# Expert weights of a mixture layer: another order of loads on SyncE's queue, w2 in runs of four rows, w1 and w3 read with a stride

## The reference

```
z      = modulate(rms_norm(tokens)) @ w_in          # S5 | differential attention | latent attention
x      = x + g_m * (concat(s5, diff, mla) @ w_out)
h      = modulate(rms_norm(x))                      # 512 tokens
group  = argmax(h @ w_group);  experts = top 2 of 8 in that group, weights w
out    = sum over the 2 experts of a token: w * ((silu(h @ w1[e]) * (h @ w3[e])) @ w2[e])
result = rms_norm(x + g_f * out)
```

## Time and profile before

| | |
|---|---|
| median of 3 runs | 1286.86 us (1285.66 to 1292.4) |
| profiled execution | 1281.67 us |
| its span, first to last instruction | 1279.9 us |
| mean granted TensorE clock | 0.888 |
| PE (TensorE matmul) busy | 960.2 us, 75% |
| PEld (weight load) busy | 453.2 us, 35% |
| DVE (VectorE) busy | 422.1 us, 33% |
| ACT (ScalarE) busy | 246.7 us, 19% |
| POOL (GpSimd) busy | 159.9 us, 12% |
| DMA moved | 264.89 MB, mean 207 GB/s |

### The profile page before, as it was taken

How to read it: one execution, slowest core, us unless ns; L and a number is a source line. 1 busy time by engine, 2 the same in 40 slices (tenths; PEclk the granted TensorE clock), 3 DMA queues, 4 the chain that set the end, 5 groups by cost and what they waited for, 6 DMA issues and landing times.

```text
span 1279.9 us, 11562 instructions
## 1 busy us (share of the span) xinstructions
PE 960.2 (75%) x3837; PEld 453.2 (35%) x3837; DVE 422.1 (33%) x1062; ACT 246.7 (19%) x529; POOL 159.9 (12%) x401
## 2 busy tenths in 40 slices
PE   4589999877999989963955577567777777777780
PEld 2245554653444544451422233222222222222220
DVE  2337656635777541350101111011111111111115
ACT  3411002123455541110100000001111111111102
POOL 5010100110000000003001100112122211121112
PEclk8799999878899999965977788789999999999985
DMA  9831211230516700040355433599999999999975
GB/s 306 309 113 60 34 66 66 38 92 7 208 56 229 133 1 16 33 148 20 148 216 218 184 123 134 222 404 392 398 392 377 376 379 406 382 341 377 392 277 202
DMA packets 61234, 264.89 MB, mean 207 GB/s; under 512 B 11496, under 2 KB 13856, under 8 KB 42256
## 3 DMA queue, kind: packets, MB, share of 16 engines
q1 hardware_dynamic: 48256, 246.04, 50.4%
q0 software_dynamic: 12768, 18.36, 5.7%
q10 hardware_dynamic: 176, 0.05, 0.0%
HBM read 266.22 MB, written 22.31 MB: 225 GB/s over the span
## 4 chain that ended last, share of the span: by engine, by line
issue 45%; PE 35%; DVE 6%; DMA 4%; POOL 4%; ACT 3%; POOLq 1%; SPq 0%; DVEq 0%; ACTq 0%
PE PS L679 9%; PE PS L906 4%; PE PS L837 3%; DMA W<-in_w_mod 3%; PE PS L814 3%; PE PS L971 2%; POOL held L526 2%; PE PS L588 2%; PE PS L638 2%; PE PS L825 1%; DVE sml L1671 1%; PE PS L747 1%; PE PS L740 1%; POOL S5R L535 1%; ACT MP L1175 1%
## 5 line engine op out<-in xcount | busy, mean ns | idle before, releaser
L968 PE MATMUL PS<-W,S5R 128*64 128x512 f32 x800 | 193.1, 628 | 63.9 <-DMA W<-in_moe_w 63.8
L679 PE MATMUL PS<-W,HTR 128*128 128x512 f32 (+2 forms) x352 | 143.9, 567 | 3.2 <-DVE MP L1398 3.2
L971 PE MATMUL PS<-W,S5R 128*128 128x512 f32 x192 | 94.4, 654 | 62.6 <-DMA W<-in_moe_w 60.2
L988 PE MATMUL PS<-W,S5R 128*64 128x512 f32 x400 | 101.9, 656 | 51.6 <-ACT S5R L1255 32.3
L968 PEld LDWEIGHTS PS<-W,S5R 128*64 128x64 f32 x800 | 57.0, 143 | 197.3 <-DMA W<-in_moe_w 99.1
L1248 ACT ACTIVATE S5R<-PS 128x256 f32<-128x256 f32 (+1 forms) x31 | 13.2, 425 | 520.5 <-PE PS L968 369.5
L679 PEld LDWEIGHTS PS<-W,HTR 128*128 128x128 f32 x352 | 66.6, 198 | 71.5 <-issue 67.9
L526 POOL TENSOR_TENSOR held<-held 1x1 f32<-1x1 f32 x147 | 26.9, 183 | 484.1 <-PE PS L953 164.3
L1905 DVE TENSOR_TENSOR S5R<-S5R,PS 128x256 f32<-128x256 f32 x25 | 10.5, 422 | 228.8 <-ACT S5R L1248 228.8
L971 PEld LDWEIGHTS PS<-W,S5R 128*128 128x128 f32 x192 | 40.0, 212 | 113.6 <-DMA W<-in_moe_w 61.8
L1917 DVE TENSOR_TENSOR S5R<-PS,QKV 64x512 f32<-64x512 f32 x50 | 34.4, 688 | 131.3 <-PE PS L988 130.5
(11 more groups left out here) (398 smaller groups left out, 1130.7 us busy)
## 6 DMA issues: line engine op xcount, KB each, us to landing
W<-in_moe_w SPq DMA_DIRECT2D x124, 1024.0 KB, 11.1
W<-in_moe_w SPq DMA_DIRECT2D x31, 2048.0 KB, 11.1
W<-in_w_mod SPq DMA_DIRECT2D x12, 2048.0 KB, 9.1
W<-in_w_in SPq DMA_DIRECT2D x3, 2048.0 KB, 10.3
QKV<-in_x SPq DMA_DIRECT2D x8, 512.0 KB, 15.4
W<-in_w_out SPq DMA_DIRECT2D x2, 2048.0 KB, 15.9
S5R<-k_d POOLq DMA_DIRECT2D x16, 128.0 KB, 5.9
xh_d<-S5R POOLq DMA_DIRECT2D x4, 512.0 KB, 2.9
```

The lines of the kernel that those rows point to most:

```text
L679: ins = mm(dst[:, c0:width], hT[:, k, tok], wslot(n, width)[:, k, c0:width], start=(k == 0), stop=(k == KD - 1))
L968: ins = mm(PS[r, 1024:1536].rearrange("p (m h) -> p m h", m=2), hgT[:, k, 0:64], w13[:, :, k, 256 * m:256 * m + 256], start=(k == 0), stop ...
L971: ins = mm(bank(2 + m), hgT[:, k, :], w13[:, m, k, :], start=(k == 0), stop=(k == KD - 1))
L988: ins = mm(PS[64 * n:64 * n + 64, 2560:3072], hidT[:, k % 2, 64 * (k // 2):64 * (k // 2) + 64], w2s[:, k, 512 * n:512 * (n + 1)], start=(k ...
```

## The change

Four edits.

1. SyncE has a loop of its own for full blocks, in which the loads of w1 and w3 for block b come before the load of w2 for block b - 1. The half blocks keep the old order. The expert number is read from `btab` once for each of the two steps.
2. `load2` gives partition p the rows 4p to 4p + 3 of w2, one run of 16 KB. The hidden features must then stand in the same order: feature 4p + k on partition p in step k. In a full block `turn_hid` reads `hid` with a stride of four. In a half block the up projection itself reads its moving operand, w1 and w3, with a stride of four elements: m = 0 takes the features with remainder 0 and 1, m = 1 those with 2 and 3; the results lie contiguously.
3. Eight of POOL's small loads wait until the modulation rows of group 0 are done.
4. The projection u goes in the order h = 0, 2, 1, 3, and each product waits only for the token tiles that it reads (four for h = 0 and 2, six for 1 and 3).

```diff
-        ztiles = [("u", h) for h in range(4)]
+        U_ORDER = (0, 2, 1, 3)
+        ztiles = [("u", h) for h in U_ORDER]
...
-                sp.dma_start(w2s, src.rearrange("e (k p) n -> p (e k) n", p=P)).then_inc(sem("w2_in"), 16)
+                sp.dma_start(w2s, src.rearrange("e (p k) n -> p (e k) n", k=4)).then_inc(sem("w2_in"), 16)
...
-            with sp.Fori(1, nblk) as b:
-                e = sp.value_load(btab[0:1, bass.ds(b, 1)], min_val=0, max_val=NE - 1)
+            def next13(b):
+                e = expert(b)
                 for piece in range(2):
                     sp.wait_ge(sem("w13_used"), 2 * b + piece - 1)
                     for m in range(2):
                         load13(e, m, piece)
+            def next2(b):
+                e = expert(b)
                 sp.wait_ge(sem("w2_used"), b)
                 load2(e)
+            next13(1)
+            with sp.Fori(2, nful + 1) as b:
+                next13(b)
+                next2(b - 1)
+            next2(nful)
+            with sp.Fori(nful + 1, nblk) as b:
+                next13(b)
+                next2(b)
...
+            pool.wait_ge(sem("mod_used"), KD // 2)
             small(GM[:, :], a["b_mod"][0][M_G * D:(M_G + 1) * D].partition_broadcast(P), "gm_in")
...
-            pe.wait_ge(sem("hT_a"), NT)
-            pe.wait_ge(sem("hT_d"), NT)
...
-            for h in range(4):
+            for h in U_ORDER:
                 dst = z_bank(("u", h))
                 t0, nt = (0, 512) if h % 2 == 0 else (512, 256)
+                pe.wait_ge(sem("hT_a"), (t0 + nt) // P)
+                pe.wait_ge(sem("hT_d"), (t0 + nt) // P)
...
-                                ins = mm(PS[r, 1024:1536].rearrange("p (m h) -> p m h", m=2), hgT[:, k, 0:64],
-                                         w13[:, :, k, 256 * m:256 * m + 256], start=(k == 0), stop=(k == KD - 1))
+                                four = w13[:, :, k, :].rearrange("p w (q f) -> p w f q", f=4)
+                                ins = mm(PS[r, 1024:1536].rearrange("p (w f q) -> p w f q", w=2, f=2), hgT[:, k, 0:64],
+                                         four[:, :, 2 * m:2 * m + 2, :], start=(k == 0), stop=(k == KD - 1))
...
-                    ins = tr(bank(4, P, k * P), hid[:, k * P:(k + 1) * P], ident)
+                    cols_k = hid[:, k * P:(k + 1) * P] if half else hid.rearrange("p (q f) -> p f q", f=4)[:, k, :]
+                    ins = tr(bank(4, P, k * P), cols_k, ident)
```

More of the change, by code:

```diff
@@ L368, in _, with expert @@
             sp.wait_ge(sem("routed"), 1)
+            nful = sp.value_load(btab[0:1, NBLK:NBLK + 1], min_val=0, max_val=NBLK - 5) + 2
             nblk = sp.value_load(btab[0:1, NBLK + 1:NBLK + 2], min_val=0, max_val=NBLK - 5) + 5
-            with sp.Fori(1, nblk) as b:
-                e = sp.value_load(btab[0:1, bass.ds(b, 1)], min_val=0, max_val=NE - 1)
+            def expert(b):
+                return sp.value_load(btab[0:1, b:b + 1] if isinstance(b, int) else btab[0:1, bass.ds(b, 1)],
+                                     min_val=0, max_val=NE - 1)
+            def next13(b):
+                e = expert(b)
                 for piece in range(2):
@@ L1401, in _ @@
             ins.then_inc(sem("bc"), 1)
-            for h in range(4):
-                dve.wait_ge(sem("z"), h + 1)
+            for n, h in enumerate(U_ORDER):
+                dve.wait_ge(sem("z"), n + 1)
                 c0, nc_ = (0, 64) if h % 2 == 0 else (64, 32)
-                cp(UT[:, h // 2, :, c0:c0 + nc_], bank(h, nc_ * CH).rearrange("p (c j) -> p j c", j=CH)).then_inc(
+                cp(UT[:, h // 2, :, c0:c0 + nc_], bank(n, nc_ * CH).rearrange("p (c j) -> p j c", j=CH)).then_inc(
                     sem("z_free"), 1)
```

## The result

| | before | after |
|---|---|---|
| median of 7 runs | 1292.05 us (1284.73 to 1293.51) | 1305.87 us (1300.04 to 1320.85) |
| profiled execution | 1281.67 us | 1305.87 us |
| its span | 1279.9 us | 1304.0 us |
| granted TensorE clock | 0.888 | 0.932 |

The ratio is 1.0115, 95% interval 1.0081 to 1.0149; it leaves out the run of 1320.85 us, which was in a slower state. The forecast was 1181 with a range of 1166 to 1240. The first rival, the doubled up projection, had said 1304.

A forecast was written before the change was run, and what follows sets the result against it. Full blocks were taken as bound by load issue order, half blocks by DMA loading. Gains of 84.2 + 15 + 0 + 5 + 1.6 = 105.8 us from 1281.67 gave 1175.9, plus 5.2 for the median: 1181, range 1166 to 1240.

The forecast's parts named there:

- The first rival: Half blocks: the stride doubles the up, TensorE becomes the bound at 21.0 us a block; 1304 us in all, chance 0.16.
- Half blocks read w1 and w3 with a stride of four: Half blocks' up projection: strided moving operand costs 0; high bound, the up doubles from 7.04 to 14.1 us.
- the 53 ns: Weight loads of transposes: 193 ns at every eighth element against 140 contiguous, read as two periods an element instead of one.
- The queue order: Full blocks: issuing w1 and w3 loads ahead of w2 removes TensorE's holes, 22.2 us a block; 82.7 us, 84.2 with clock.
- the third rival: Full blocks: late gathers or second pieces of w1 and w3 replace the hole, five blocks lose 35 us; 1216, chance 0.04.
- w2 in long runs: Half blocks: w2 as one run of 16 KB a partition loads faster, 15 us taken from a possible 22.
- The start: Before the expert blocks: delaying eight small loads saves 5 us, reordering the projection u saves 1.6 us.

The follow-up runs named there:

- e5: The changed kernel with full blocks too reading w1 and w3 with a stride of four elements, one product over all 128 columns at a time; 1402.76 us in a single run.
- e2: The changed kernel with half blocks taking columns as pairs of neighbours out of every four and turning hid with a stride of two; 1188.34 us, ratio 0.9219 to before.
- e1: The changed kernel with its second edit undone: w2 in four runs of 4 KB a partition, contiguous reads of w1 and w3; 1192.85 us, ratio 0.9241 to before.
- e3: The changed kernel with contiguous w1 and w3 reads in half blocks, features ordered by eight small turns of hid, w2 in 16 KB runs; 1189.72 us, ratio 0.9216 to before.
- e6: The kernel before with the new order of loads on SyncE's queue as the only edit; 1208.4 us, ratio 0.9383.
- e9: The kernel before with the second edit only: w2 in one 16 KB run a partition, stride of four in half blocks, old load order; 1399.93 us, ratio 1.0848.

## Why the prediction was wrong

**The step that failed.** In "Half blocks read w1 and w3 with a stride of four" the term was taken as 0, with 7.04 us more per half up as its high bound. It measured 7.5 us more per half up and, after what DMA had hidden is taken off, 113.5 us in the sum. The argument was that a float32 column is read once and held for both of its periods, so that a read every two periods is fast enough. The runs showed the opposite side of that fork: the lone strided stream of e5 and the paired ones both doubled. What is shown is 1.77 ns for each column of a record with one element to a line (14.52 us for 16 pairs of 512 columns), against 0.86 ns contiguous (7.04 us). That the array reads each column twice would explain it and is an inference.

The pace that spoke for 0 came from weight loads, and the runs show that they were no measure of the moving side. The transposes of `hid`, whose weight loads take 140 ns when contiguous, read it with a stride of four elements in the full blocks of the changed kernel and with a stride of two in the half blocks of e2 (columns as in rows 8; the full blocks of after, then the half blocks of e2):

```profile
L1002 PEld LDWEIGHTS PS<-CST,S5R x24: 195/208/220, 611.2 to 722.3; 128*128 128x128 f32 x24
```

```profile
L1002 PEld LDWEIGHTS PS<-CST,S5R x48: 194/208/219, 765.8 to 1148.4; 128*128 128x128 f32 x48
```

Both take 208 ns, more than the 193 of a stride of eight, though a stride of two puts two elements on each line; and the contiguous weight loads of L993, no transposes, take 190 ns. So the 53 ns that the prediction read as one extra period an element are not the price of a new line, and that they matched the pace of float32 columns was a coincidence. Without them only the two contiguous streams that did not slow each other spoke for the 0.

**The rule of the Trainium skill.** By the Trainium skill ("SBUF — State Buffer", "Door 1: The DMA port swizzle") at least two hits on a 16-byte line give full bandwidth and a new line for every access pays. For the moving operand the runs agree with both halves: 612 ns against 592 with two hits, 1079 with one. For the weight loads of transposes they do not: 208 ns against 140 with two hits as with one. The prediction's sentence that the trace agrees for the weight loads does not hold.

**The rival was right in size.** It said half blocks of 21.0 us and 108 us more; measured 21.3 and 113.5. Its condition, a half up beyond 13.4 us, was met at 14.5. That its total of 1304 us came within 2 us of 1305.87 is in part luck: against the trace of before it said 17 us more and 24.1 came, and the 5.2 us between trace and median, which it added, were not there in the changed kernel's runs. A chance of 0.16 was too little for a case for which the rule of the Trainium skill spoke, against a mechanism that no row showed.

**The queue order.** Right: 22.0 us a block for 22.2, 83.5 us for 82.7, and no other wait in the hole's place. The gather that the third rival feared shows no wait before L976 in the loop; the 22.9 us before the first of them, at 590.75, stood there before the change too (22.8).

**w2 in long runs.** 15 us were taken; some 4 us by the mean of three traces of each kind, not clear of their spread, is what the runs show. The term rested on one stretch of 3 us at 360 GB/s; over 360 us of half blocks e1 and e3 differ by 2 GB/s in 385. One window that short was no mean. In the changed kernel itself the term was nothing, since DMA no longer was the bound.

**The start.** 6.6 us were said; 7.4 came against the trace of before, 10.6 against e6 and e9. The split into 5 and 1.6 is not measured: the single gains change by 3.2 us with the trace they are read against.

**The measurement.** The profiled execution of before lies 10 us below the median of its seven runs, that of after on its median. The difference of medians, 13.8 us, is therefore smaller than the 24.1 of the spans, and the account of the two traces is right to some 10 us only. Of these, 3.2 lie before the query projection. The half blocks' part is firm: from up(6) to the start of the last down pass 432.3, 432.7 and 433.8 us in before, e1 and e6, and 545.8, 547.4 and 549.6 in after, e9 and e5.

## What to carry to other kernels

A float32 moving operand may be strided if two elements fall on each 16-byte line; a stride of four elements doubles the matmul, with one stream or two. A layout that needs another order of features can take neighbours in pairs, or sort them in a small turn. Here both were hidden behind the loads: e2 and e3 ran at 0.922 of the time before. When several edits go together and one of them has no row behind it, price it alone: here it ate all that the others gave. A row of one operand's side, here the weight loads, does not price the other. And before a gain of a few us is read from one trace, look whether a second trace of the same code has the same times there.

## What the runs showed of the hardware

- A record of 512 float32 columns took 592 ns contiguous, 612 with two elements to a 16-byte line (in pairs or with a step of two), 1079 with one.
- The same penalty falls on a lone stream over 128 columns of the array (28.9 us for 13.9) and on two beside each other over 64 each (14.5 for 7.04).
- The weight loads of float32 transposes took 140 ns contiguous, 208 with a stride of two (e2) or four (after), 193 with a stride of eight; there two elements to a line did not help.
- Runs of 16 KB instead of 4 KB moved w2 hardly faster: 386 (e3) against 384 GB/s (e1) over 360 us at a DMA share of 0.98.
- The same 64 records of the projection u took 20.9 us at a granted clock of 1.00 and 24.0 at 0.87, and unchanged code before them reached the query projection at 83.24 us in one trace and 86.44 in two.
